# A piece of the next gate product between an expert's up and down product, and page numbers loaded once per pair

## What is computed

```python
# attention of the new tokens over 1024 cached keys and values, fetched by page number
k_past = cache_k[i][page_table].reshape(bs, past, SB_HEADS, SB_HEAD_DIM)
v_past = cache_v[i][page_table].reshape(bs, past, SB_HEADS, SB_HEAD_DIM)
...
# experts: every token has two of 16; d = 1024, an expert's width is 512
hg = jnp.einsum('td,edf->tef', t, w_gate)
hu = jnp.einsum('td,edf->tef', t, w_up)
act = jax.nn.silu(hg) * hu * combine[..., None].astype(t.dtype)
return jnp.einsum('tef,efd->td', act, w_down).reshape(b, L, d)
```

## Time and profile before

| | us |
|---|---|
| timed runs, median of 3 | 1128.38 |
| lowest and highest of them | 1127.12 and 1129.35 |
| profiled execution, its own time | 1124.03 |
| its span in the trace | 1122.3 |
| mean granted TensorE clock in it | 0.921 of full |

### The profile page before, as it was taken

The page is one execution under the profiler, slowest core; times in us unless marked ns, Lnnn a source line. Parts: engine busy times, 40 slices in busy tenths (PEclk is TensorE's granted clock), DMA queues, the critical chain, the costliest instruction groups (busy, mean ns, idle before and its releaser), DMA issues.

```text
span 1122.3 us, 12426 instructions
## 1 busy us (share of the span) xinstructions
PE 947.8 (84%) x4149; PEld 688.6 (61%) x4149; DVE 645.9 (58%) x1206; ACT 447.1 (40%) x665; POOL 39.3 (4%) x75
## 2 busy tenths in 40 slices
PE   5899999999888687765699966989998999899685
PEld 3476776777554445432467755777777777677363
DVE  2329993001335545423647347788877787888574
ACT  0221102213122233122422044767766776677542
POOL 4000004000000000000000010000000000001100
PEclk9899999999859798897899976999999999999988
DMA  8042355332220676676303241877787788688501
GB/s 226 1 150 98 127 185 181 115 114 75 79 72 10 192 240 221 215 236 260 115 29 134 75 149 67 317 284 303 313 309 291 290 322 319 257 318 309 199 1 47
DMA packets 58069, 203.33 MB, mean 181 GB/s; under 512 B 8761, under 2 KB 9081, under 8 KB 51863
## 3 DMA queue, kind: packets, MB, share of 16 engines
q1 hardware_dynamic: 49280, 185.19, 45.5%
q10 hardware_dynamic: 6031, 9.19, 3.1%
q0 software_dynamic: 2704, 8.27, 2.3%
HBM read 188.96 MB, written 14.03 MB: 181 GB/s over the span
## 4 chain that ended last, share of the span: by engine, by line
PE 45%; DVE 9%; SPq 6%; issue 4%; ACT 4%; DMA 0%; DVEq 0%; POOL 0%; ACTq 0%
PE bank L1957 10%; PE bank L1959 10%; PE bank L1958 10%; PE bank L1948 5%; SPq L345 3%; SPq L348 3%; PE bank L2043 2%; PE bank L1879 2%; PE bank L2149 1%; PE bank L1844 1%; PE bank L2067 1%; DVE act_lo L1505 1%; PE bank L1797 1%; DVE h_tok L1360 1%; PE bank L1853 1%
## 5 line engine op out<-in xcount | busy, mean ns | idle before, releaser
L1669 PE MATMUL bank<-scratch,ring 128*128 128x320 f32 x896 | 242.5, 433 | 0.0
L1669 PEld LDWEIGHTS bank<-scratch,ring 128*128 128x128 f32 x896 | 169.8, 190 | 70.6 <-issue 0.5
L1454 DVE TENSOR_TENSOR pieces<-ring,pieces 128x1024 fp32r<-128x1024 f32 x144 | 173.3, 1222 | 43.3 <-ACT pieces L592 40.7
L592 ACT ACTIVATE pieces<-ring 128x1024 fp32r<-128x1024 f32 x144 | 150.8, 1060 | 76.7 <-PE bank L1959 70.2
L592 ACT ACTIVATE proj<-bank 128x512 f32<-128x512 f32 (+4 forms) x73 | 36.3, 506 | 157.5 <-PE bank L1669 117.0
L1081 DVE SCALAR_TENSOR_TENSOR proj<-scratch,par_w,proj 128x256 f32<-128x256 f32 x240 | 73.7, 380 | 1.1
L1957 PE MATMUL bank<-pieces,act_ft 128*128 128x512 f32 x96 | 43.0, 448 | 28.6 <-DVE act_lo L1505 28.6
L1454 DVE TENSOR_TENSOR last_piece<-ring,last_piece 128x1024 fp32r<-128x1024 f32 x48 | 58.6, 1221 | 2.3 <-ACT last_piece L592 0.3
L592 ACT ACTIVATE scratch<-bank 128x512 f32<-128x512 f32 (+5 forms) x42 | 20.5, 520 | 97.1 <-PE bank L1879 42.1
L592 ACT ACTIVATE last_piece<-ring 128x1024 fp32r<-128x1024 f32 x48 | 51.0, 1062 | 13.7 <-PE bank L1959 13.7
L1844 PE MATMUL bank<-ident,ring 128*128 128x128 f32 x256 | 38.3, 315 | 13.6 <-ACT proj L592 6.4
(11 more groups left out here) (384 smaller groups left out, 1665.1 us busy)
## 6 DMA issues: line engine op xcount, KB each, us to landing
ring<-in_w_expert_gate SPq DMA_DIRECT2D x16, 2048.0 KB, 7.9
ring<-in_w_expert_up SPq DMA_DIRECT2D x16, 2048.0 KB, 8.2
ring<-in_w_expert_down SPq DMA_DIRECT2D x16, 2048.0 KB, 7.8
ring<-in_w_in SPq DMA_DIRECT2D x14, 2048.0 KB, 7.8
ring<-in_cache_k SPq DMA_DIRECT2D x64, 256.0 KB, 3.2
ring<-in_cache_v SPq DMA_DIRECT2D x64, 256.0 KB, 3.1
moe_rows<-att ACTq DMA_DIRECT2D x16, 512.0 KB, 4.5
ring<-in_w_branch SPq DMA_DIRECT2D x3, 2048.0 KB, 9.9
```

The costliest lines, as they stand in the source:

```text
L592: return F(out, in_, ACT.Copy)
L1454: TT(piece_of[r % 4][:, 1, :], raw_piece(EXPERTS + 3 * e, r), piece_of[r % 4][:, 0, :].bitcast(F32), ALU.subtract).then_inc(s("lo_ready"), 1)
L1669: m = MM(bank[t % 4][:, 0:T], slot(j, DC, GROUP)[:, k, (t % 4) * P:(t % 4 + 1) * P], h[:, k, :], start=k == 0, stop=k == DC - 1)
```

## The change

1. Experts, order on TensorE: the step of expert e begins with its up product (bank 4), since its gate product was done in the step before. Then come both gathers, piece 0 of the gate product of e + 1 (bank 3), the turn of act (now into bank 4), gate piece 1, the down product, gate pieces 2 and 3. Before the first step stands the first expert's gate product by itself, with its last gather after the first piece. The last expert has up and down product only.
2. The pieces' order on ScalarE and VectorE follows: `stream(r)` says which load and which quarter of it is piece r of a step (up 0 to 3, gate' 0 and 1, down 0 to 3, gate' 2 and 3). On ScalarE `y_copy` moves behind the first high half of a step, silu behind the third, and both `h_hi` ahead of act_ft. On VectorE both `h_rest` move behind act_lo. The product act is no longer strided.
3. Loads: the ring's order is gate 0, up 0, then per step gate of e + 1, down of e, up of e + 1. Each waits for the slot's pieces: gate for the up pieces of e - 1, down for all of the gate pieces of e (with the last low half of the step before), up of e + 1 for the down pieces of e - 1. Gate 1 and down 0 are issued only once `crowded` is known.
4. Down weights are laid out by chunks: a partition holds row p of each block of 128 (four runs of 4 KB) and not four rows in a row (16 KB).
5. Page numbers: `page_numbers(i)` loads 16 registers per pair ahead of the K fetches of that pair, and K and V fetches use them. The loop over pairs on SP is written out.

```diff
+        def stream(r):
+            return (0, r) if r < 4 else (1, r - 4) if r < 6 else (2, r - 6) if r < 10 else (1, r - 8)
+        def last_stream(r):
+            return (0, r) if r < 4 else (1, r - 4)
...
+            def page_numbers(i):
+                return [sp.value_load(pages[0:1, bass.ds(2 * NPAGE * i + p, 1)], min_val=0, max_val=POOL - 1)
+                        for p in range(2 * NPAGE)]
+            def fetch(which, numbers, u, hf, to, loaded_):
                 dst = slot(to, NPAGE, W)
-                some = range(4 * hf, 4 * hf + 4)
-                regs = [sp.value_load(pages[0:1, bass.ds(i * (2 * NPAGE) + (u * NPAGE + p), 1)], min_val=0, max_val=POOL - 1)
-                        for p in some]
...
+            for i in range(1, NB // 2):
+                after = page_numbers(i)
                 for hf in range(2):
-                    fetch_k(i + 1, hf)
-                fetch_v(i)
+                    fetch_k(i, after, hf)
...
+                if i > 1:
+                    sp.wait_ge(s("o_done"), i - 1)
+                    for u in range(2):
+                        for hf in range(2):
+                            fetch("v", now, u, hf, 2 + u, f"v_loaded{u}")
+                now = after
...
+                rows_of = "e (p k) n -> p (e k) n" if r < 2 else "e (k p) n -> p (e k) n"
...
+                def up_free(i, n):
+                    return "lo_ready", i * (4 * PIECES) + (PIECES * n + 8)
+                def gate_free(i, n):
+                    return "lo_ready", i * (4 * PIECES) + (PIECES * n + 16)
+                def down_free(i, n):
+                    return "lo_ready", i * (4 * PIECES) + (PIECES * n + 14)
+                def step_loads(i, n, gate=True):
+                    expert(STEP + 3 * n + 1, i * 4 + (n + 1), 0, up_free(i, n - 1))
+                    expert(STEP + 3 * n + 2, i * 4 + n, 2, gate_free(i, n - 1))
+                    expert(STEP + 3 * n + 3, i * 4 + (n + 1), 1, down_free(i, n - 1))
...
@@ ScalarE, turn: for each expert e @@
+                        hi(i, e, 0, final)
                         if not (first and e == 0):
                             y_copy(n + (-1), first=first and e == 1)
-                        hi(i, e, 4)
+                        hi(i, e, 1, final)
...
+                        hi(i, e, 2, final)
                         act.wait_ge(s("piece_used"), n * PIECES + (4 - PIECES))
                         F(silu_s, bank[3][:, :], ACT.Silu).then_inc(s("silu_ready"), 1)
-                        for r in range(8, 12):
-                            hi(i, e, r)
-                        act.wait_ge(s("act_turned"), n)
-                        copy(act_ft[:, :], bank[3][:, :]).then_inc(s("act_hi_ready"), 1)
+                        hi(i, e, 3, final)
+                        for r in range(4, 8):
+                            hi(i, e, r, final)
                         if not end:
                             for j in range(2):
                                 h_hi(i, e // 2 + 1, e % 2 * 2 + j)
-                        for r in range(0 if last and e == 3 else 4):
-                            hi(i, e + 1, r)
+                        act.wait_ge(s("act_turned"), n)
+                        copy(act_ft[:, :], bank[4][:, :]).then_inc(s("act_hi_ready"), 1)
+                        for r in range(8, 8 if final else 12):
+                            hi(i, e, r)
...
@@ VectorE, the same @@
+                        for r in range(1, 6):
+                            lo(i, e, r, final)
...
+                        TT(act_s, bank[4][:, :], silu_s, ALU.mult).then_inc(s("act_ready"), 1)
+                        for r in range(6, 8):
+                            lo(i, e, r, final)
                         dve.wait_ge(s("act_hi_ready"), n)
+                        TT(act_lo[:, :], bank[4][:, :], act_ft[:, :].bitcast(F32), ALU.subtract).then_inc(s("act_f_ready"), 1)
+                        if not final:
+                            for r in range(8, 12):
+                                if not end and r < 10:
+                                    h_rest(i, e // 2 + 1, e % 2 * 2 + r - 8)
+                                lo(i, e, r)
...
@@ TensorE, the same @@
+                        for r in range(4):
+                            features(i, e, bank[4], r, done + (r + 1), False)
                         if not end:
-                            gather(i, pair + 1, 2 * u)
+                            for j in range(2):
+                                gather(i, pair + 1, 2 * u + j)
+                        if not final:
+                            pe.wait_ge(s("silu_ready"), n)
+                            features(i, e + 1, bank[3], 0, done + 5, True)
                         pe.wait_ge(s("act_ready"), n)
                         for k in range(DE // P):
-                            m = TR(bank[3][:, k * P:(k + 1) * P], act_s[:, k * P:(k + 1) * P], ident[:, :])
+                            m = TR(bank[4][:, k * P:(k + 1) * P], act_s[:, k * P:(k + 1) * P], ident[:, :])
                         m.then_inc(s("act_turned"), 1)
-                        if not end:
-                            gather(i, pair + 1, 2 * u + 1)
+                        if not final:
+                            features(i, e + 1, bank[3], 1, done + 6, True)
                         pe.wait_ge(s("act_f_ready"), n)
...
+                        if not final:
+                            for r in range(2, 4):
+                                features(i, e + 1, bank[3], r, done + (9 + r), True)
```

More of the change, by code:

```diff
@@ L351, in fetch_k @@
-            def fetch_k(i, hf):
-                for u in range(2):
[L353 to L360, removed]
+                for p in range(4 * hf, 4 * hf + 4):
+                    sp.dma_start(dst[:, p, :], a["cache_" + which][0][bass.ds(numbers[u * NPAGE + p], 1)].rearrange(
+                        "n s h d -> (n s) (h d)")).then_inc(s(loaded_), 16)
@@ L362, in _, with fetch_k @@
+            def fetch_k(i, numbers, hf):
+                for u in range(2):
+                    sp.wait_ge(s("k_page_turned"), 16 * i + 8 * hf + 4 * u + 4 - 16)
+                    fetch("k", numbers, u, hf, u, f"k_loaded{hf}{u}")
             sp.wait_ge(s("proj_done"), 56)
+            now = page_numbers(0)
             for hf in range(2):
                 for u in range(2):
[L365 to L370, removed]
@@ L410, in _, with last_loads @@
             first = [("branch_done", 2 * DC), ("branch_done", 3 * DC), ("out_done", 5), ("out_done", 6)]
-            for n in range(4):
-                expert(EXPERTS + n, n // 3, n % 3, first[n])
-            def experts(sems):
+            for n in range(2):
+                expert(EXPERTS + n, 0, n, first[n])
+            def last_loads(frees):
+                L = EXPERTS + 3 * NE
+                for j, (sem_, v) in enumerate(frees):
+                    sp.wait_ge(s(sem_), v)
+                    if j == 0:
+                        ring_load(L, slot(L % 4, PLE // P, D), a["w_ple_proj"][0].rearrange("(k p) n -> p k n", p=P))
+                    elif j < 3:
+                        ring_load(L + j, slot((L + j) % 4, DC, GROUP), halves(a["w_ple_gate"], j - 1))
+                    else:
+                        ring_load(L + 3, slot((L + 3) % 4, D), a["norm_final"].unsqueeze(0).broadcast_to((P, D)))
@@ L425, in turn @@
                         expert(EXPERTS + n, i * 4 + e, r, free(r, i, back))
+                for n in (2, 3):
+                    expert(EXPERTS + n, n // 3, n % 3, first[n])
                 turn(0, 4)
@@ L428, in experts @@
                     turn(i, 0)
[L430 to L446, removed]
+                last_loads((free(0, 0, NE - 1), free(1, 0, NE), free(2, 0, NE), free(0, 0, NE)))
         @block.gpsimd
@@ L860, in _, with hi @@
             with act.If(act.value_load(crowded[:, :], min_val=0, max_val=1) == 0):
[L861 to L868, removed]
+                def hi(i, e, r, final=False):
+                    which, k = last_stream(r) if final else stream(r)
+                    if k == 0:
+                        loaded(act, STEP + 3 * e + which, i, 12)
+                    n = PIECES * e + r + 4
+                    act.wait_ge(s("piece_used"), i * (4 * PIECES) + (n - 3))
+                    copy(piece_of[r % 4][:, 0, :], raw_piece(STEP + 3 * e + which, k)).then_inc(s("hi_ready"), 1)
                 def h_hi(i, pair, j):
```

111 lines of the change are left out of this document (62 added, 49 removed).

## The result

| | before | after |
|---|---|---|
| timed runs, median | 1127.75 (4 runs) | 1098.74 (4 runs) |
| lowest and highest | 1123.25, 1129.35 | 1096.47, 1100.83 |
| profiled execution | 1124.03 | 1100.83 |

The ratio is 0.976, with a 95% interval of 0.973 to 0.979: faster by 29 us in the medians. The profiled execution of after took as long as the slowest of its four, that of before lies 3.7 us under its median, so between the two traces there are only 23.2 us to be found.

The account below looks back on a forecast made before the run. TensorE's order of work was taken to set the end nearly everywhere, so its waits matter. Experts 25 us and attention 6 make 31 us saved: 1093 us by the profiled execution, 1097 as median, forecast 1088 to 1105 (0.60), range 1084 to 1114.

Parts of the forecast that it names:

- The chain from turn to down product: Expert step: shortest chain 2.07 us, 1.78 covered by TensorE's work, so a wait of 0.3 to 0.5 us stays.
- The loop 11.05 + D: Expert step: VectorE 6.85 us, the down load's time, ScalarE 3.45, act_ft 0.60, hand-overs 0.15; the step can't be shorter.
- The signs that I named: Experts: act_lo waits 0.3 to 1.2 us, down loads land in 9 to 10, steps 20.6; attention: no cache_v wait over 1.1.
- D = 9.6: Experts: a down load takes 9.6 us from issue to landing, 9.1 plus 0.5 for the store; bounds 7.8 and 10.6.
- the 9.1: Earlier trace: the first of two 2 MB loads issued directly one after the other took 9.1 us; base for the down load.
- 4 KB runs at nothing: Down weights in four 4 KB runs a partition, not one of 16 KB: no further cost, at worst 1 us a load.
- The rule of the Trainium skill: Rival, expert loads in ring order: down load stays at 7.8 to 8.3 us, TensorE rules, 1086 us; chance 0.15.
- TensorE's 19.9: Expert step by TensorE alone: twelve pieces, two gathers, the turn's loading and the remaining wait, 19.8 to 19.9 us.
- The steps of experts 15 and 16: Expert 15 has no gathers, h_hi or h_rest: 17.5 us; the last, without cover, up to its down product: 16.8.
- The clock: Experts: 10 us lost at 1.2 instead of 2.4 GHz; the sum takes 2.4 everywhere and gives 2 us back.
- Experts in all: Between first and last down product 331.3 us become 303.9; 0.3 lost ahead, 2 given back: 25 us saved.
- Attention: Page numbers loaded once a pair: 4.0 us of V page waits and 2 of clock saved, 6 us, bounds 0 and 7.4.

Follow-up runs that it names:

- the loop cut: The changed kernel with the down weights' load in two halves, the first issued some 12 us earlier: 1076.49 us, ratio 0.956 to the kernel before.
- store_late: The changed kernel with the 512 KB store of an expert's rows issued after the eighth high half, not the second: 1077.16 us, ratio 0.957.
- experiment 5: The kernel before with one edit, VectorE's act_lo moved ahead of the first h_rest (the swapped kernel): 1094.72 us against 1127.26, ratio 0.972.

## Why the prediction was right, point by point

The forecast was 1097 us and the median is 1098.74; but the terms were not as right as their sum. The path was right, the loop through the down load; the sizes on it were not.

- *The chain from turn to down product, 2.07 us, with 0.3 to 0.5 left.* Right, where it could be seen: 0.2 us with the loop cut, 0.23 and 0.41 in the swapped kernel. In the changed kernel another chain hid it.
- *The loop 11.05 + D and that it decides.* Right. The rows give 10.9 + D, and cutting it gave 22 us. The signs that I named came only in part: ScalarE waits for the down weights and the V pages are in time, but the loads land after 9.8 to 11.5 us and not 9 to 10, the steps are 20.7 to 22.4 us (23.4 where row_numbers() runs) and not 20.6, and the waits for act_lo are 0.9 to 3.0 us and not 0.3 to 1.2.
- *D = 9.6.* The mean is 10.2, which is 13 x 0.6 = 8 us of the sum. What failed is how D was put together: 1.3 us for an up load behind it, taken from the 9.1 of the earlier trace rows, and 0.5 for the store. The runs show 0 for the up load (7.9 with it and no store, 10.0 with the store and without it) and 2.2 for the store. The two errors nearly cancelled. What delayed the 9.1 load was not tried and stays open; its neighbour had 2 KB runs, the up load has 16 KB.
- *4 KB runs at nothing.* Wrong by 1.4 us of D beside a store (10.1 against 8.7), and right without one. These 1.4 are part of the store's 2.2, not a second term.
- *The rule of the Trainium skill ("DMA: Bandwidth & Descriptors", section "Queues, rings and completion order") that one queue's loads go in order.* I gave its result 0.15. The rule agrees with store_late (7.9 with a load behind), and I was wrong to let the 9.1 speak against it. Its consequence, TensorE's 19.9, still didn't come, because the store goes by another queue, of which the same section speaks too.
- *The steps of experts 15 and 16, 17.5 and 16.8.* They took 20.05 and 19.18. For the first I took off 1.6 us of h_rest, but the h_rest that follow the act_lo of expert 14 are on this loop; TensorE waited 2.96 us for act_lo there. The last step ran at a mean clock of 0.88 behind that wait, and my sum for it was short besides: with the load cut, at full clock, it still takes 17.55. Together 4.9 us of the sum.
- *The clock.* I left 2 us; the window's 0.98 is 6 us. Waits of 0.9 to 3.0 us stayed, and so did stretches at 1.2 GHz; in the kernels where all but the last experts' waits are 0.2 to 0.4 us the window rounds to 1.00. These 6 us are inside the steps as measured and are no term beside them: the 13 steps took 278.0 us instead of 267.8 + 1.8, 8.4 more, the last two 4.9 more, and less the 2 us given back that is 11.3, the whole distance from the 305.9 forecast to 317.2.
- *Experts in all:* 25 us forecast, 14 by the traces. *Attention:* 6 forecast, 8.8 by the traces and 8.9 by the runs. The waits went as forecast, to the copy's 0.97 us; mis-sized was the clock behind them, of which I took 2 of 3.4 us, and 1.2 us more came from K turns at full clock (6.62 to 5.43).
- By the traces the sum was 31 us and is 23: 1093 was forecast for the profiled execution, and it took 1100.83. By the medians it is 29. So part of the agreement is luck: the attention part came out larger than forecast and the expert part smaller, and the one profiled execution of each kernel lies at the other end of its spread.

What I missed altogether stands in experiment 5. I read from the earlier trace rows that act_lo stood behind h_rest, and took the change's own cure, cover on TensorE, for the only one.

## What to carry to other kernels

When an engine waits, look at what stands ahead of the released instruction on the releasing engine before you look for cover: here one swapped line gave twice what the reordering of three engines gave. When loads are moved, write down the loop from buffer release through load to the next release, and add it up; if it is near the step of the bounding engine, a transfer on another queue, a store of a quarter of the size, can decide which of the two is the bound. And price such a load from a row that has the same company, not from the nearest row of the same size.

## What the runs showed of the hardware

- A store of 512 KB on ScalarE's queue, issued some 1.2 us behind, held up a 2 MB load in 4 KB runs on SP's queue by 2.2 us (7.9 to 10.1), one in 16 KB runs by 0.9 (7.8 to 8.7); the store took 8.3 us beside the first and 11.1 beside the second. A store of twice the size added 0.7 us more.
- A second 2 MB load issued 0.6 us behind the first on the same queue didn't delay it: 7.9 us, beside 7.8 for a load alone in the earlier trace rows. A load issued while the one before it on the queue had 2.1 us to go, with the store behind it, took 11.3 us.
